# Two experts' blocks woven together in the mixture-of-experts layer of a two-layer decoder

## The reference, cut to what matters

```python
def moe_swiglu(xn, w_router, w_gate, w_up, w_down):
    logits = (xn @ w_router).astype(jnp.float32)
    top_v, top_i = lax.top_k(logits, TOP_K)              # TOP_K = 2 of 8
    top_w = jax.nn.softmax(top_v, axis=-1)
    gates = jnp.sum(jax.nn.one_hot(top_i, N_EXPERTS) * top_w[..., None], axis=-2)
    out = jnp.zeros_like(xn)
    for e in range(N_EXPERTS):
        ye = (silu(xn @ w_gate[e]) * (xn @ w_up[e])) @ w_down[e]
        out = out + gates[..., e:e + 1] * ye
    return out
```

## Time and profile before

| what | value |
|---|---|
| time, median of 3 runs | 1368.06 us (1367.66 to 1368.17) |
| the profiled execution | 1368.13 us |
| its span, first to last instruction | 1366.4 us |
| TensorE busy | 1325.6 us (97%) |
| VectorE busy | 1154.0 us (84%) |
| ScalarE busy | 951.8 us (70%) |
| read from HBM | 420.27 MB |

### The profile page before, as it was taken

One profiled execution on the slowest core, in us unless ns is written; L12 is line 12 of the kernel. 1 busy time (PEld: TensorE's weight loads), 2 busy tenths in 40 slices (PEclk: granted clock), 3 DMA queues, 4 the chain that ended last, 5 costly groups with the idle time before them and its releaser, 6 DMA issues.

```text
span 1366.4 us, 17261 instructions
## 1 busy us (share of the span) xinstructions
PE 1325.6 (97%) x6404; PEld 1082.8 (79%) x6404; DVE 1154.0 (84%) x970; ACT 951.8 (70%) x874; POOL 71.5 (5%) x110
## 2 busy tenths in 40 slices
PE   8999999999999999999999999999999999999998
PEld 7776888888877887777777777888888888888887
DVE  6897655556889989999999999998898899889886
ACT  5676544446777777777777777777777777776775
POOL 2120910000200000000000000000000000000000
PEclk9999999999999999999999999999999999999999
DMA  8743765555299889999999999999999999999980
GB/s 305 266 130 89 256 203 195 185 185 162 86 357 347 317 323 359 393 395 393 394 393 390 380 394 395 394 372 371 337 351 375 377 349 359 376 337 359 358 329 31
DMA packets 197860, 422.46 MB, mean 309 GB/s; under 512 B 13064, under 2 KB 37392, under 8 KB 197776
## 3 DMA queue, kind: packets, MB, share of 16 engines
q1 hardware_dynamic: 197776, 421.35, 85.2%
HBM read 420.27 MB, written 1.05 MB: 308 GB/s over the span
## 4 chain that ended last, share of the span: by engine, by line
PE 74%; DVE 16%; ACT 5%; issue 3%; SPq 1%; DMA 1%; POOL 0%; ACTq 0%; DVEq 0%; POOLq 0%
PE ps L334 19%; PE ps L336 19%; PE ps L335 19%; DVE w_lo L314 12%; PE ps L885 5%; ACT w_hi L297 4%; PE ps L883 3%; PE ps L1048 1%; PE ps L865 1%; PE ps L1023 1%; PE ps L1049 1%; PE ps L862 1%; PE ps L882 1%; DMA raw<-in_attn_w_qkv_dram 1%; PE ps L1042 1%
## 5 line engine op out<-in xcount | busy, mean ns | idle before, releaser
L314 DVE TENSOR_TENSOR w_lo<-raw,w_hi 128x2048 fp32r<-128x2048 f32 x382 | 867.8, 2290 | 128.6 <-ACT w_hi L297 127.4
L297 ACT ACTIVATE w_hi<-raw 128x2048 fp32r<-128x2048 f32 x385 | 732.6, 1914 | 122.2 <-PE ps L336 100.0
L334 PE MATMUL ps<-w_hi,xe 128*128 128x512 f32 x448 | 178.4, 398 | 3.0 <-DVE w_lo L314 2.9
L336 PE MATMUL ps<-w_hi,xe 128*128 128x512 f32 x448 | 174.8, 390 | 0.0
L335 PE MATMUL ps<-w_lo,xe 128*128 128x512 f32 x448 | 174.5, 390 | 0.0
L334 PE MATMUL ps<-w_hi,h_t_hi 128*128 128x512 f32 x360 | 141.4, 393 | 0.5 <-DVE w_lo L314 0.5
L336 PE MATMUL ps<-w_hi,h_t_lo 128*128 128x512 f32 x360 | 140.3, 390 | 0.0
L335 PE MATMUL ps<-w_lo,h_t_hi 128*128 128x512 f32 x360 | 140.2, 389 | 0.0
L334 PE MATMUL ps<-w_hi,xb 128*128 128x512 f32 x280 | 111.4, 398 | 1.9 <-DVE w_lo L314 1.9
L885 PE MATMUL ps<-a_all,w_hi 128*128 128x512 f32 x308 | 109.8, 396 | 0.0
L336 PE MATMUL ps<-w_hi,xb 128*128 128x512 f32 x280 | 109.2, 390 | 0.0
(11 more groups left out here) (319 smaller groups left out, 1856.9 us busy)
## 6 DMA issues: line engine op xcount, KB each, us to landing
raw<-in_moe_w_gate_dram SPq DMA_DIRECT2D x112, 1024.0 KB, 7.6
raw<-in_moe_w_up_dram SPq DMA_DIRECT2D x111, 1024.0 KB, 7.4
raw<-in_moe_w_down_dram SPq DMA_DIRECT2D x111, 1024.0 KB, 7.4
raw<-in_attn_w_qkv_dram SPq DMA_DIRECT2D x11, 1024.0 KB, 12.6
raw<-in_ffn_w_gate_dram SPq DMA_DIRECT2D x11, 1024.0 KB, 5.3
raw<-in_ffn_w_up_dram SPq DMA_DIRECT2D x11, 1024.0 KB, 5.3
raw<-in_ffn_w_down_dram SPq DMA_DIRECT2D x11, 1024.0 KB, 5.0
raw<-in_ple_w_gate_dram SPq DMA_DIRECT2D x8, 1024.0 KB, 6.9
```

The lines of the kernel that those rows point to most:

```text
L297: nc.scalar.activation(w_hi[:, u % SPLIT, :], raw_slot(u), ACT.Copy).then_inc(hi_ready, 1)
L314: nc.vector.tensor_tensor(w_lo[:, u % SPLIT, :], raw_slot(u), w_hi[:, u % SPLIT, :].bitcast(F32), ALU.subtract).then_inc(lo_ready, 1)
L334: nc.tensor.matmul(out, x[0], w[0], start=first, stop=False)
L336: return nc.tensor.matmul(out, x[1], w[0], start=False, stop=last)
```

## The change

Turn 0 and the last turn keep one expert. The six turns between become three *pairs*, a small expert (e=0) and a large one (e=1), and a pair goes block by block: block 0 of the small one, block 0 of the large one, block 1 of the small one and so on. In the second fence below the first `pair` is ScalarE's and the second VectorE's. The places are given by `ROOM`, so the three small experts are at 1, 3 and 5. The down units in a block are those of the same expert's block before, which is now two blocks back; the transposition of a block's hidden values comes behind G1 of the next block. On ScalarE the silu comes behind the high part of D1, and on VectorE `hiddens` behind the fourth low part. The first block of the first pair has four units, and the first block of the last turn has eight. The two experts' down results have PSUM banks of their own (6 and 7, 3 and 4); all scatters use bank 5, one quarter at a time, set between units by the tables `SCATTERS` and `LAST_SCATTERS`. Gathering goes in four pieces (banks 5 and 2). ScalarE copies the transposed picks, which VectorE did. If an expert has more tokens than its room, more turns follow, as before (11 places are kept for them instead of 8, so the arrays of sorting and placing grow from 8 to 19 places).

TensorE's `pair` and what it calls:

```diff
+ROOM = (SLOTS, FEW, SLOTS, FEW, SLOTS, FEW, SLOTS, SLOTS)
...
-RANK_AT = (0, 5, 6, 7, 1, 2, 3, 4)
-FEW_AT = (1, 2, 3)
+RANK_AT = (0, 5, 1, 6, 2, 7, 3, 4)
+PLACES = NE + len(SECOND)
...
+        PIECE_BANKS = (5, 2, 5, 2)
+        PAIR_BLOCKS = [(f, e) for f in range(FB) for e in range(2)]
+        SCATTERS = {(0, 1, 1): (-1, 0), (0, 1, 3): (-1, 1), (0, 1, 5): (-1, 2), (1, 0, 1): (-1, 3),
+                    (1, 0, 5): (0, 0), (1, 1, 1): (0, 1), (1, 1, 3): (0, 2), (1, 1, 5): (0, 3)}
...
             def scatter(q, t, k=0):
 
                 pe.wait_ge(y_lo_ready, t + 1 + k)
...
+                pe.wait_ge(pick_t_copied, t % 2 + t + 1 + k)
+                pe.wait_ge(added, 4 * t + q + 4 * k)
...
+            def pair(k, first=False):
+
+                for f, e in PAIR_BLOCKS:
+                    few, x, g = e == 0, (xe, xb)[e], block_at_seq(f, e)
+                    bare = first and f == 0 and e == 0
+                    u = pair_unit(f, e, first)
...
+                    for n in range(2):
+                        for half in range(2):
+                            if f == 0 and e == 0 and n == 0:
+                                pe.wait_ge(xe_lo_ready, 2 * half + 4 + 2 * k)
+                            gate_or_up(u + 2 * n + half, n, half, x, g, k, few)
+                            if n == 0 and half == 0:
...
+                                transpose_hidden(g - 1, k, few=e == 1)
+                            if f == 3 and e == 0 and n == 1 and half == 0:
+                                transpose_picks(k, 2)
+                            if f == FB - 1 and e == 1 and n == 1:
+                                gather_piece(half, k + 2, g + FB * k)
+                            between(2 * n + half)
+                    if bare:
+                        continue
+                    if f == 1:
+                        if e or not first:
+                            pe.wait_ge(y_lo_ready, e + k)
+                    f_down, g_down = (f - 1) % FB, g - 2
+                    t_down = e + 1 if f else e - 1
+                    down(u + 4, f_down, 0, g_down, t_down, k, few=few)
+                    if f == FB - 1 and e == 1:
+                        gather_piece(2, k + 2, g + FB * k)
+                        gather_piece(3, k + 2, g + FB * k)
+                    down(u + 5, f_down, 1, g_down, t_down, k, few=few)
+                    between(5)
```

Then ScalarE's and VectorE's order, and TensorE's calls:

```diff
+            def pair(k, first=False):
+
+                for f, e in PAIR_BLOCKS:
+                    g, u = block_at_seq(f, e), pair_unit(f, e, first)
+                    for n in range(4 if first and f == 0 and e == 0 else 6):
+                        split_hi(u + n + AHEAD, k)
...
+                        if n == 1:
+                            hidden_hi(g - 1, k, few=e == 1)
+                        if n == 2:
+                            silus(g, u + 1, k)
...
+            def pair(k, slots, first=False):
+
+                for f, e in PAIR_BLOCKS:
...
+                    for n in range(4 if bare else 6):
+                        split_lo(u + n + AHEAD, k)
...
+                        if n == 1:
+                            hidden_lo(g - 1, k, few=e == 1)
+                        if n == 3:
+                            hiddens(g, u + 3, k)
+                        if (f, e, n) in SCATTERS:
+                            t, q = SCATTERS[f, e, n]
+                            if not (first and t < 0):
+                                add_result(q, t, k)
...
-            turn(1, 0, few=True)
-            turn(2, 0, few=True, few_before=True)
-            turn(1, 2, few=True, few_before=True)
-            turn(2, 2, few_before=True)
+            pair(0, first=True)
+            pair(2)
             with pe.Fori(3, pairs + 1) as it:
-                turn(1, (it - 1) * 2)
-                turn(2, (it - 1) * 2)
-            turn(1, turns - 1, end=True)
+                pair((it - 1) * 2)
+            last_turn(turns - 1)
```

More of the change, by code:

```diff
@@ L146, in trunk @@
         more = sb("more", [P, 2], I32)
[L147 removed]
+        order = sb("order", [P, PLACES], I32)
         with nc.sbuf_tensor("o_scratch", [P, 512], F32) as o_scratch:
@@ L1066, in down, with gate_or_up @@
                 last.then_inc(unit_used, 1)
[L1068 to L1073, removed]
+            def gate_or_up(u, n, half, x, g, k=0, few=False):
+                unit(u, k)
+                if half == 0:
+                    pe.wait_ge((silu_ready, hidden_ready)[n], g + FB * k)
+                for c in range(4):
+                    d, w = 4 * half + c, weights(u, c, 0, 512, 512)
+                    if few and n == 1:
+                        both = x[:, 2 * d * P + FEW:2 * d * P + FEW + P]
+                        last = product_few(ps[:, n, :], both, w, d == 0, d == KD - 1)
+                    else:
+                        rows = x[:, 2 * d * P:(2 * d + 1) * P], x[:, (2 * d + 1) * P:(2 * d + 2) * P]
+                        last = product(ps[:, n, :], rows, w, d == 0, d == KD - 1)
+                last.then_inc(unit_used, 1)
@@ L1075, in turn, with transpose_picks, first_turn @@
+            def transpose_picks(k, experts):
+                pe.wait_ge(added, 4 + 4 * k)
+                for e in range(experts):
+                    for tt in range(TT):
+                        at = (e * TT + tt) * P
+                        last = nc.tensor.transpose(ps[:, 5, at:at + P], pick_of(e, tt).bitcast(F32), ident[:, :])
+                last.then_inc(pick_transposed, experts)
+            def first_turn():
                 for f in range(FB):
-                    u, g = turn_unit(t0, f), JF + FB * t0 + f
@@ L1077, in turn @@
-                    for n, freed in ((0, silu_ready), (1, hidden_ready)):
+                    u, g = turn_unit(0, f), JF + f
+                    gather = f == FB - 1
+                    for n in range(2):
                         for half in range(2):
[L1079 to L1094, removed]
@@ L1115, in turn @@
[L1115 to L1119, removed]
+                    if f:
+                        down(u + 4, f - 1, 0, g - 1, 0)
+                        if gather:
+                            gather_piece(2, 0, g)
+                            gather_piece(3, 0, g)
+                        down(u + 5, f - 1, 1, g - 1, 0)
+                        if not gather:
+                            transpose_hidden(g)
@@ L2212, in _ @@
+            pair(0, iota_few[:, :], first=True)
+            pair(2, iota_few[:, :])
             with dve.Fori(3, pairs + 1) as it:
-                turn(1, (it - 1) * 2)
-                turn(2, (it - 1) * 2)
-            turn(1, turns - 1, end=True)
+                pair((it - 1) * 2, iota_next)
+            last_turn(turns - 1)
             split_lo(U_TURN + AHEAD, turns)
```

525 lines of the change are left out of this document (326 added, 199 removed).

## The result

The changed kernel takes 1382.99 us (median of 4 runs, 1381.55 to 1383.36) against 1368.07 (4 runs) on the same chip: ratio 1.0104, interval 1.0092 to 1.0116. It is slower by about 15 us. 1380.9 was predicted, with 1371 to 1390 as range.

What follows compares the result with a forecast made beforehand. Small blocks were taken as bound by a chain through rings of three slots, large ones by TensorE's own time. 1368.13 + 11.1 (pairs) + 0 (DMA, turn changes) + 1.7 (turn 0) = 1380.9 us, range 1371 to 1390.

Steps and rivals of the forecast that it cites:

- The steady pair: Small plus large block, 21 times: 9.38 + 23.52 = 32.90 us against 32.37 before, so +11.1 us.
- the silu leaves the chain: Small block's stretch from G2's release to next G1: silu behind D1's high part, 9.38 us, 0.41 less than 9.79.
- the fold is open work: TensorE, small block's fold behind the large block's G1: nothing hides it, 0.94 us in each pair.
- The predicted waits: TensorE waits for low parts ahead of D1 (about 1 us), D2 and, new, the large G1 (0.8 to 1.0).
- DMA: Weight loads: a pair wants 382 GB/s, under the queue's 394; nothing gained or lost, loads land in 6 to 8 us.
- Changes between turns: Scatters, picks' transpositions, gatherings and waits in turns 1 to 7: 31.8 us carried over unchanged, bounds 24 and 42.
- rival C: Changes between turns wait: each of 21 scatters waits 0.5 us for its single bank, 1391 us; chance 0.11.
- Turn 0: Sorting and placing over 19 places and new operations on VectorE: +1.7 us, bounds 0 and 1.7.
- The larger sort: VectorE in turn 0, 19 places instead of 8: three sorting operations +0.27 and one more of 0.2, placing +0.72 us.
- A: TensorE stops waiting in the pairs and the load queue's 394 GB/s decides: 1335 us; chance 0.06.
- B: Fold hidden in a wait because VectorE is later with G2's low part by 0.6 to 1.5 us: 1361; chance 0.07.

Runs made afterwards that it cites:

- 20 folds moved: Changed kernel with the small expert's transposition and fold ahead of G1 in 20 of 21 large blocks, not the first pair's first: 1364.48 us, ratio 0.9973.
- filled waits: Changed kernel with 40 small useless matmuls around the transposition of turn 0's second block, where TensorE waited: 1381.65 us, ratio 1.0098.
- the small sort: Changed kernel with sorting and placing over 8 places, constants for the 11 overflow places: 1379.72 us, ratio 1.0080.
- all folds first: Changed kernel with the small block's fold put back between its D2 and the large block's G1, in all pairs: 1369.48 us, ratio 1.0001.
- both: Changed kernel with the fold ahead of G1 in 20 of 21 large blocks and sorting over 8 places: 1363.15 us, ratio 0.9958.
- the last kernel: Changed kernel with fold ahead of G1 in 20 large blocks, sorting over 8 places, filled waits, turn 0's silu behind D1's high part: 1360.69 us, ratio 0.9941.

## Why the prediction was right, and where a term was off

*The steady pair* was predicted at 32.90 us and took 32.95, 16.59 + 16.36. Its two halves are right one by one: D1's high part to the next G1 took the 9.38 worked out, and the rest 23.57 against 23.52. That the silu leaves the chain is shown by the run with it back (+0.36 a pair, 0.41 expected). That the fold is open work is shown by the run in which it is not: 20 folds moved gave 17.7 us in the pairs' windows, and 17.1 to 17.7 between executions with a mean clock of 1.000 (1381.55 against 1363.84 to 1364.48); the medians' 18.5 has part of the clock in it. The predicted waits are there too. TensorE's rows in a pair without the picks' transposition:

```profile
676.91 0.50 PE L1111 MATMUL ps<-w_hi,p_t_hi 128*128 128x512 f32 x1 [0.77 <-DVE w_lo L324]
...
679.20 0.50 PE L1111 MATMUL ps<-w_hi,p_t_hi 128*128 128x512 f32 x1 [0.18 <-DVE w_lo L324]
...
682.00 0.50 PE L344 MATMUL ps<-w_hi,xb 128*128 128x512 f32 x1 [0.69 <-DVE w_lo L324]
```

These waits are counted from the modelled end of the matmul before. From start to start, less 0.227, the three are 0.93, 0.34 and 0.86 us, 2.1 together, which is the 9.38 - 7.3 of the prediction: about 1 us ahead of D1 and 0.8 to 1.0 ahead of the large G1, as said. In the pair shown first, D1's wait is 0.30 instead of 0.77, because the picks' transposition fills it, and that pair is no longer for it.

*DMA*: gate loads of the changed kernel at 600 to 620 us and at 900 to 920 us:

```profile
raw<-in_moe_w_gate_dram SPq DMA_DIRECT2D x2, 1024.0 KB, 7.2
```

```profile
raw<-in_moe_w_gate_dram SPq DMA_DIRECT2D x3, 1024.0 KB, 6.9
```

The lag of the earlier trace rows is gone, and the queue moves 382 GB/s, as said. Nothing was gained by it, as said.

*Changes between turns* were carried over at 31.8. Turns 1 to 7 took 840.74; 21 x 32.95 and seven large blocks of 16.8 are 809.6, which leaves 31.2. The term was carried over, not derived, so its agreement holds for the total and says little of the parts. What TensorE waited for in turns 1 to 7 is low parts, never VectorE's addition that the single bank needs; rival C is out.

*Turn 0* was predicted at +1.7 and took +3.42. This term was mis-sized, and in two parts. The larger sort was nearly right: VectorE's sorting takes 3.51 us, 0.47 more than before, as worked out, and placing 2.97 instead of 1.58, as its rows show:

```profile
423.57 0.47 DVE L2276 TENSOR_TENSOR tmp<-place,tmp 128x304 f32<-128x304 f32 x1
...
425.82 0.29 DVE L2284 TENSOR_TENSOR tmp<-iota_few,iota_slot 128x128 f32<-128x128 f32 x1
426.15 0.35 DVE L2285 SCALAR_TENSOR_TENSOR tmp<-tmp,iota_slot 128x128 f32<-128x128 f32 x1
426.54 2.29 DVE L324 TENSOR_TENSOR w_lo<-raw,w_hi 128x2048 fp32r<-128x2048 f32 x1
```

That is 1.86 us, and turn 0 shows 1.93 of it (101.14 with filled waits, less 99.21): nothing hides it, and the lower bound of nothing was never near. The other 1.5 us are TensorE's clock, which the prediction took as full throughout. In the timeline of the changed kernel:

```profile
408.46 0.39 PE L346 MATMUL ps<-w_hi,h_t_lo 128*128 128x512 f32 x1
409.43 0.65 PE L932 MATMUL ps<-ident,tmp 128*128 128x128 f32 x4 [0.59 <-DVE tmp L2071]
411.63 0.79 PE L344 MATMUL ps<-w_hi,xe 128*128 128x512 f32 x1 [1.55 <-DVE w_lo L324]
412.22 0.63 PE L345 MATMUL ps<-w_lo,xe 128*128 128x512 f32 x1
412.65 0.63 PE L346 MATMUL ps<-w_hi,xe 128*128 128x512 f32 x1
```

Behind two waits matmuls come 0.43 apart instead of 0.23. The wait of 1.55 was there before, as long, with no such fall in the one profile; the one ahead of it was about 0.1 and is 0.59 now. The fall is there with the small sort too, where that wait is 0.3. So 1.5 us of the difference between the two profiled executions are the clock's. It isn't in every execution of the changed kernel: the one of four with a mean clock of 1.000 can't have had it. Nor is a lower clock the change's alone: of 30 executions of the kernel before that were run beside the first eight experiments, eight have a mean of 0.998 or 0.997 and took 1369.1 to 1371.1 us, where those at 1.000 took 1367.4 to 1368.8 (and one 1370.0). Where in those executions it fell, no profile shows.

*The whole*: 11.1 predicted for the pairs and the turns' changes against 11.5, 1.7 against 3.4 in turn 0; with 0.3 ahead of the experts, 15.2 against 12.8. The median is 2.1 us above the prediction, the execution with a mean clock of 1.000 (1381.55) 0.65. Little cancels in this: the one term that came out under its forecast is the turns' changes, by 0.6 us.

*The rivals.* A (TensorE stops waiting, 1335) never came near: a pair stays at 32 us even with the fold hidden. B was out for the order given, since VectorE isn't late with G2's low part; but its mechanism is real: put the fold where there is a wait, and the same woven order is faster than the kernel before.

## What to carry to other kernels

When an order is changed, list what stood inside waits before. The fold cost nothing where it was, beside a low part that TensorE had to wait for, and its full 0.94 us a pair behind the next unit, though it is the same work. A change of several moves is worth undoing one by one: here the late silu was a gain and could be had alone, with one line moved, and it beat the whole change.

## What the runs showed of the hardware that was not expected

**Half the clock for 3.4 us behind two short waits.** The same order of turn 0 and the same two waits (0.59 and 1.55 us) ran with and without the fall of the clock, which gives its price. Windows of 412 to 414 us in the changed kernel and in the one with 20 folds moved (busy TensorE with its matmuls first, the granted clock third from the end):

```profile
412.00:414.00 2.00, 2.00 (x6) 1.52 (x6) 2.00 (x2) 0.52 (x1) 0.00 (x0) 0.50 0.66 162
```

```profile
412.00:414.00 2.00, 2.00 (x9) 1.63 (x10) 2.00 (x2) 0.81 (x1) 0.00 (x0) 1.00 0.48 99
```

Six matmuls against nine. The block was 20.05 us long with half the clock, for 3.41 us of it, and 18.58 without: 1.47 us. The Trainium skill's page TensorE: Matmul & The Clock Gate (Terms) takes the penalty as the throttled time multiplied by one less the granted share, an estimated 3.41 x 0.5 = 1.7 us; the blocks show a little less.

What decides stays open. Of the seven profiles of kernels with the new turn 0 and unfilled waits, five show the fall (the changed kernel, and those with the silu early, all folds first, the smaller sort, and both) and two don't (the product behind the fifth low part, and 20 folds moved). The second wait is 1.54 or 1.55 us in all seven; the first is 0.58 or 0.59, and 0.3 in the two with the smaller sort, which both show the fall. The three with filled waits don't show it, which agrees with standing still as its cause; three profiles can't prove it where two of seven do without. The executions without a profile say that it is a matter of the single execution: four of five with the smaller sort had a mean clock of 1.000. A mean of 0.999 doesn't prove the fall, though; the fastest execution of the last kernel (1360.5 us) has it.

**The loads' lag is a loan with a term.** With 414 GB/s wanted and 394 moved, gate loads took 7.2 us to land at 500 to 520 us and 13.5 at 700 to 720, and the first wait for one came at 699 us, some 200 us into the small turns; at 800 to 820 they took 13.8. A stage measured early would have shown no limit at all.
